# Sum of squares in the recurrent branch's output norm: fp32r products on split squares in place of plain fp32 products

## The chip, the cores and the metric

One core of a Trainium2 chip runs the whole program. The metric is the device time of one execution in microseconds; the median over the runs is given. The engines are TensorE (PE in the profile, its weight loads PEld), VectorE (DVE), ScalarE (ACT), GpSimd (POOL) and SyncE (SP), which only issues DMAs here. They run side by side and wait for each other by semaphores; within one engine, instructions run in the order in which they are written.

## The reference, cut to what matters

The model is a decoder trunk of width 1024 over 1024 positions. Layer 0 mixes with two head groups side by side: windowed attention (A) and gated linear attention (B, the recurrent branch, 4 heads of width 128). The change touches the norm on B's output:

```python
def rms_norm(x, g):
    xf = x.astype(jnp.float32)
    y = xf * lax.rsqrt(jnp.mean(xf * xf, axis=-1, keepdims=True) + EPS)
    return (y * g.astype(jnp.float32)).astype(x.dtype)
...
    ob = gla(split_heads(qb, N_HEADS_B), split_heads(kb, N_HEADS_B),
             split_heads(vb, N_HEADS_B), split_heads(log_a, N_HEADS_B))
    ob = rms_norm(ob, g_out_b) * jax.nn.silu(split_heads(rb, N_HEADS_B).astype(jnp.float32))
```

The mean runs over the 128 channels of one head. This happens once per execution, for 4 heads.

## The kernel before, in words

All activations lie transposed: 128 channels on the partitions, 1024 positions along the row. The large projections split both operands into a high fp32r part and a low rest, and make each product of 512 columns out of three fp32r products (high by high, low by high, high by low; `cross` for whole tiles, `half_tile` for half tiles). ScalarE or GpSimd makes the high part, VectorE or GpSimd the low one. Weights come by DMA into `w_raw` and GpSimd splits them, one tile of 128x1024 after the other: L594 writes `w_hi`, L597 writes `w_lo`. There are two slots for split tiles, so the split of tile n+2 starts when TensorE has ended its products with tile n.

Branch B works on two heads at a time (`bp` 0, then 1; `h` 0 and 1 within it). For each pair TensorE projects k, q, v (twice) and r (twice), and in between makes the gates, the running sums of the decay ("cum"), transposes of the decayed keys ("kd") and of v ("vt"), states ("kv"), scores ("att"), outputs ("o") and the sums of squares ("ss"). The list `B_SEQ` fixes that order and gives each result one of four PSUM slots of two banks; `slot_free` makes TensorE wait until VectorE has taken what lay in the slot before. So `b_project("r", 1, 1)`, which uses slot 3, waits until `take_gate(1, 0)` has taken the result of `b_project("r", 1, 0)` from slot 3.

The norm runs so: VectorE copies the output out of PSUM (`take_bo`, L1560), ScalarE squares it (`b_square`, L2186) into `b_v` (h = 0) or `b_att` (h = 1), TensorE multiplies a 128x128 matrix of ones with the squares (`out_squares`, L946), which leaves each position's sum on all partitions; VectorE scales it (`out_var`, L1565), ScalarE takes the logarithm and the exponential for a first guess of the root (`b_guess`, `b_root`), and VectorE refines it in steps (`out_step`: L1573, L1577, L1579), then applies gain and gate (L1582, L1586).

For pair 0, TensorE's order around it is: `chunk_out(0)`, `b_project("v", 1, 0)`, `gate(1)`, `out_squares(0, 0)`, `out_squares(0, 1)`, `b_project("v", 1, 1)`, `cumulate(1)`, `b_project("r", 1, 0)`, `kd_transposes(1)` (L886), `bv_transposes` twice (L893), `b_project("r", 1, 1)`. `kd_transposes(1)` waits for `b_kd` (L1510), which VectorE makes in `decays(1)` after `log_sigmoid(1)`, `out_var`, `log_decay(1)`, six steps of `out_step` and `take_bv(1, 1)`:

```python
                dve.wait_ge(B.e, 6 * bp + 3)
                dve.tensor_tensor(b_kd[:], b_k[bp][:], b_e[:], ALU.mult).then_inc(B.dec, 1)

                dve.wait_ge(B.dec, 6 * bp + 2)
                dve.tensor_tensor(chunks(b_e[:]), chunks(b_cum[:]), at(b_cum[:], CH // 2 - 1), ALU.subtract).then_inc(B.dec, 1)
                take_gate(bp, 0)
```

For pair 1, branch A's first head pair is woven in: its projections are 50 "pieces" (0 to 15 make v, 16 and 17 transpose it, 18 to 25 make the first half of k, "K0", 26 to 33 the first half of q, "Q0", 34 to 41 and 42 to 49 the second halves "K1" and "Q1"). A piece of a projection is three products of 512 columns (L1028, L1029, L1030). Before, the squares of pair 1 stand between pieces 33 and 34, and `scores(0)`, the first attention scores, between pieces 41 and 42; `scores(0)` waits until `out_var(1, 1)` has emptied the slot. VectorE's order there is `take_bo(1, 0)`, `take_bo(1, 1)`, `take_part(0, Q0)` (rotates Q0 and splits it, L1650 to L1665; it waits for piece 33), `out_var(1, 0)`, `out_var(1, 1)`, then the first step on K1.

Of the kernel before, what the change touches and what calls it, by code (L numbers as in the profile page):

```python
# [22 lines left out]
F32 = mybir.dt.float32  # L23
F32R = mybir.dt.float32r
# [69 lines left out]
def build(nc, xT, pos, consts, logmul, gains, wgu, bgu, wgl, w_in, w_out, w_u, w_v, w_outc, wsT, bsp,  # L94
          w_up, w_dn, conv, outT):
    with ExitStack() as ctx:
        arena = -(-nc.sbuf_base // 64) * 64

        def sb(name, kb, shape, dt=F32):
            return nc.alloc_sbuf_tensor_at(name, shape, dt, offset=arena + int(kb * 1024))  # L100

        def sem(name):
            return ctx.enter_context(nc.semaphore(name))
# [10 lines left out]
        acc = sb("acc", 180, [P, S])  # L114
        cst = sb("cst", 200, [P, C_N])
        gain = sb("gain", 202.25, [P, G_N])
        ones = sb("ones", 202.5, [P, P])
        cw = sb("cw", 203, [P, 2, 2 * FT, 4])
        tiny = sb("tiny", 204.5, [P, 64])
        carry = sb("carry", 204.75, [P, 4])  # L120
# [43 lines left out]
        b_st = sb("b_st", 144, [P, NCH, P])  # L164
        b_att = sb("b_att", 172, [P, S])
        b_v = sb("b_v", 180, [P, S])
        wgu_sb = sb("wgu_sb", 205, [P, 256])
        wgl_raw = sb("wgl_raw", 188, [P, KT, 16])
        wgl_both = sb("wgl_both", 206, [P, KT, 48], F32R)
# [60 lines left out]


        s_wgl = sem("w_gl_split")
        s_eps = sem("eps_written")

        class Bsem:
            def __init__(self):
                self.ready = sem("b_result_ready")
                self.free = sem("b_result_taken")
                self.silu = sem("b_silu")
                self.gl = sem("b_gl_projected")  # L240
                self.glt = sem("b_gl_taken")
                self.min = sem("b_min")
                self.e = sem("b_exp_ln")
                self.la = sem("b_log_decay")
                self.dec = sem("b_decay_steps")
                self.state = sem("b_state")
                self.zero = sem("b_scores_zeroed")
                self.osq = [sem("b_out0_squared"), sem("b_out1_squared")]
                self.oe = [sem("b_out0_ln_exp"), sem("b_out1_ln_exp")]
                self.o = [sem("b_out0_steps"), sem("b_out1_steps")]  # L250
        B = Bsem()
# [204 lines left out]
        def _(sp):  # L456
# [11 lines left out]
            sp.dma_start(cw[:], conv).then_inc(s_tab, 16)  # L468
            sp.dma_start(pos_i[:], pos.partition_broadcast(P)).then_inc(s_tab, 16)
            sp.dma_start(lmul[:], logmul).then_inc(s_tab, 16)  # L470
            sp.wait_ge(s_setup, 2)
            sp.dma_start(wgu_sb[0:16, :], wgu).then_inc(s_tab, 16)
            sp.dma_start(wgu_sb[32:48, :], wgu).then_inc(s_tab, 16)
            sp.dma_start(wgu_sb[48:49, :], bgu).then_inc(s_tab, 16)
# [238 lines left out]
        def b_out(kind, bp, a=0):  # L713
            slot = B_SEQ[b_index(kind, bp, a)][3]
            return ps[:, 2 * slot:2 * slot + 2, :].rearrange("p b n -> p (b n)")
# [95 lines left out]
        def _(pe):  # L811
# [128 lines left out]

            def out_squares(bp, h):
                slot_free("ss", bp, h)
                pe.wait_ge(B.osq[h], bp + 1)
                t = b_v if h == 0 else b_att
                for c in range(2):
                    ins = pe.matmul(b_out("ss", bp, h)[:, c * HALF:(c + 1) * HALF], ones[:], t[:, c * HALF:(c + 1) * HALF],  # L946
                                    start=True, stop=True)
                ins.then_inc(B.ready, 1)


# [197 lines left out]
            for j in range(16, 26):  # L1148
                piece(0, j)
            chunk_out(1)  # L1150
            for j in range(26, 34):
                piece(0, j)
            out_squares(1, 0)
            out_squares(1, 1)
            for j in range(34, 42):
                piece(0, j)
            pe.wait_ge(*b_taken(len(B_SEQ) - 1))
            scores(0)
# [234 lines left out]
        def _(dve):  # L1393
# [30 lines left out]
                                         act_hi[:, k, :].bitcast(F32), ALU.mult, ALU.subtract).then_inc(norm.lo.sem, 1)  # L1424

            dve.memset(ones[:], 1.0).then_inc(s_setup, 1)
            dve.memset(tiny[:, 61:62], EPS).then_inc(s_eps, 1)
            dve.memset(wgu_sb[0:32, :], 0.0).then_inc(s_setup, 1)
            dve.memset(glT[32:64, :], 1.0).then_inc(s_rope_v, 1)
            for k in range(KT):  # L1430
# [30 lines left out]
            def reduce_angles():  # L1461
                for part in PI_PARTS:
                    step(dve.scalar_tensor_tensor(r_a[:], r_n[:], -part, r_a[:], ALU.mult, ALU.add))
                step(dve.tensor_scalar(r_a[:], r_a[:], 3.1415925, -3.1415925, ALU.min, ALU.max))
# [23 lines left out]
            def take_bv(bp, h):  # L1488
                if bp:
                    dve.wait_ge(*b_count("vt", bp - 1, 1))  # L1490
                dve.tensor_tensor(b_vt[:, h, :], ready("v", bp, h), rstd[:], ALU.mult).then_inc(B.free, 1)
# [67 lines left out]
            def take_bo(bp, h):  # L1559
                dve.tensor_copy((b_k if h == 0 else b_q)[bp][:], ready("o", bp, h)).then_inc(B.free, 1)  # L1560

            def out_var(bp, h):

                v = out_variance(h)
                dve.tensor_scalar(v, ready("ss", bp, h), 1.0 / P, EPS, ALU.mult, ALU.add).then_inc(B.free, 1)  # L1565

            def out_step(bp, h, step):

                v, y, o = out_variance(h), out_guess(bp, h), (b_k if h == 0 else b_q)[bp]
                c0 = 5 * bp  # L1570
                if step == 0:
                    dve.wait_ge(B.oe[h], 2 * bp + 2)
                    dve.scalar_tensor_tensor(v, v, -0.5, y, ALU.mult, ALU.mult).then_inc(B.o[h], 1)  # L1573
                    return
                dve.wait_ge(B.o[h], c0 + step)
                if step == 1:
                    dve.tensor_tensor(v, v, y, ALU.mult).then_inc(B.o[h], 1)  # L1577
                elif step == 2:
                    dve.scalar_tensor_tensor(y, v, 1.5, y, ALU.add, ALU.mult).then_inc(B.o[h], 1)  # L1579
                elif step == 3:  # L1580
                    dve.wait_ge(B.osq[h], bp + 1)
                    dve.scalar_tensor_tensor(o[:], o[:], gain[:, G_OUT:G_OUT + 1], y, ALU.mult, ALU.mult).then_inc(B.o[h], 1)  # L1582
                else:
                    dve.wait_ge(B.silu, 2 * bp + h + 1)
                    r = oT[:, 4 + 2 * bp + h, :]
                    dve.tensor_tensor(r, o[:], r, ALU.mult).then_inc(B.o[h], 1)  # L1586
# [19 lines left out]
            take_bo(0, 0)  # L1606
            take_bo(0, 1)
            reduce_angles()
            take_bv(1, 0)
            log_sigmoid(1)  # L1610
            out_var(0, 0)
# [111 lines left out]
            take_bo(1, 0)  # L1723
            take_bo(1, 1)
            take_part(0, Q0)
            out_var(1, 0)
            out_var(1, 1)
            take_part(0, K1, (0,))
# [407 lines left out]
        def _(act):  # L2136
# [46 lines left out]

            def b_square(bp, h):
                act.wait_ge(*b_taken(b_index("o", bp, h)))
                act.activation((b_v if h == 0 else b_att)[:], (b_k if h == 0 else b_q)[bp][:], ACT.Square  # L2186
                               ).then_inc(B.osq[h], 1)

            def b_guess(bp, h):
                act.wait_ge(*b_taken(b_index("ss", bp, h)))  # L2190
# [155 lines left out]
            def ffn(F, layer, norm, nxt, last):  # L2346
# [107 lines left out]
                silu(FT - 1)  # L2454
                for t in range(4, STEPS):
                    if last and t == ITEM_AT[0] - 3:
                        act.wait_ge(s_eps, 1)
                        act.activation(tiny[:, 62:63], tiny[:, 61:62], ACT.Abs_reciprocal_sqrt).then_inc(s_preload, 1)
                    d_high(t)
                    if t in ITEM_AT:  # L2460
                        i = ITEM_AT.index(t)
                        if last:
                            act.wait_ge(*past(F.dsum, len(SUMS)))
                            act.wait_ge(*past(F.xadd, tile_done(0, HALF_TILES[0][i])))
                            half_square(f1, 0, i)
                        else:
                            item(0, i)
# [134 lines left out]
```

## Time and profile before

| | before |
|---|---|
| median of 3 runs | 2119.1 us (2119.04 to 2119.45) |
| the profiled execution | 2119.03 us; its span, first to last instruction, 2117.2 us |
| mean granted TensorE clock | 0.997 |
| TensorE busy | 2091.2 us, 99% of the span |
| VectorE busy | 1467.6 us, 69% |
| ScalarE busy | 881.0 us, 42% |
| GpSimd busy | 885.6 us, 42% |

The busy time of an engine is the sum of its instructions' durations with overlaps counted once. The profiled execution is one run of its own; it lies 0.07 us under the median, so sums made on its trace can be set against the median as they stand. The squares of pair 0 stand near 140 us of the span and those of pair 1 near 219 us.

### The profile page before, as it was taken

How to read it: one execution, taken by the hardware profiler on the slowest of the kernel's cores; microseconds unless marked ns; L12 is line 12 of the kernel's file. 1: busy time of each engine (PE TensorE's matmuls, PEld its weight loads, DVE VectorE, ACT ScalarE, POOL GpSimd, SP SyncE). 2: the span in 40 equal slices, each digit the busy share in tenths (PEclk: the TensorE clock that was granted, in tenths of full speed). 3: DMA queues.
4: the chain of work that ended last, by engine and by line, in shares of the span. 5: the costliest groups of instructions: out<-in, count | busy, mean ns of one | idle time of the engine just before them, and what ended most of it. 6: DMA issues, size and time to landing. Idle time of an engine off the chain costs nothing.

```text
span 2117.2 us, 26181 instructions
## 1 busy us (share of the span) xinstructions
PE 2091.2 (99%) x10190; PEld 1709.3 (81%) x10190; DVE 1467.6 (69%) x1631; ACT 881.0 (42%) x1154; POOL 885.6 (42%) x459
## 2 busy tenths in 40 slices
PE   8999999999999999999999999999999999999997
PEld 6888777778888888888888888888888888888886
DVE  7669855554986677667899604437966676686988
ACT  4231344453554444444435431215544444444444
POOL 4333221223488767770001333434877768730000
PEclk9999999999999999999999999999999999999999
DMA  4101000021422222117984111213222222239872
GB/s 170 41 30 41 30 23 19 21 80 61 146 93 80 90 90 80 70 70 251 389 300 163 60 41 41 60 40 119 81 89 90 90 72 78 90 124 384 306 279 80
DMA packets 95100, 236.10 MB, mean 112 GB/s; under 512 B 10081, under 2 KB 12418, under 8 KB 94978
## 3 DMA queue, kind: packets, MB, share of 16 engines
q1 hardware_dynamic: 93106, 229.70, 30.5%
q10 hardware_dynamic: 1872, 4.74, 0.6%
q8 instruction: 81, 1.33, 0.3%
q14 instruction: 41, 0.34, 0.0%
HBM read 198.75 MB, written 35.65 MB: 111 GB/s over the span
## 4 chain that ended last, share of the span: by engine, by line
PE 90%; DVE 6%; issue 2%; ACT 2%; DMA 0%; POOL 0%; SPq 0%; DVEq 0%; ACTq 0%; POOLq 0%
PE ps L1228 12%; PE ps L1229 12%; PE ps L1230 12%; PE ps L1262 7%; PE ps L1264 7%; PE ps L1265 7%; PE ps L818 5%; PE ps L821 5%; PE ps L824 5%; PE ps L1028 2%; PE ps L1030 2%; PE ps L1029 2%; PE ps L1133 2%; PE ps L1098 1%; PE ps L1333 1%
## 5 line engine op out<-in xcount | busy, mean ns | idle before, releaser
L594 POOL TENSOR_TENSOR w_hi<-w_raw,ones 128x1024 fp32r<-128x1024 f32 x56 | 115.6, 2065 | 746.4 <-PE ps L824 232.1
L1228 PE MATMUL ps<-t_hi,w_hi 128*128 128x512 f32 x672 | 264.1, 393 | 1.6 <-ACT snap L2365 1.3
L1229 PE MATMUL ps<-t_lo,w_hi 128*128 128x512 f32 x672 | 262.0, 390 | 0.0
L1230 PE MATMUL ps<-t_hi,w_lo 128*128 128x512 f32 x672 | 261.6, 389 | 0.0
L1262 PE MATMUL ps<-d_hi 128*128 128x512 f32 (+1 forms) x640 | 244.6, 382 | 0.7 <-DVE d_lo L1941 0.7
L1264 PE MATMUL ps<-d_lo,d_hi 128*128 128x512 f32 (+1 forms) x640 | 243.9, 381 | 0.0
L1265 PE MATMUL ps<-d_hi,d_lo 128*128 128x512 f32 (+1 forms) x640 | 243.9, 381 | 0.0
L645 POOL TENSOR_TENSOR w_lo<-w_sum,w_hi 128x1024 fp32r<-128x1024 f32 x84 | 232.3, 2776 | 25.2 <-ACT w_hi L2368 25.2
L645 POOL TENSOR_TENSOR w_lo<-w_raw,w_hi 128x1024 fp32r<-128x1024 f32 x84 | 157.5, 1875 | 172.1 <-ACT w_hi L2368 158.3
L1228 PE MATMUL ps<-act_hi,w_hi 128*128 128x512 f32 x504 | 196.2, 389 | 0.0
L1229 PE MATMUL ps<-act_lo,w_hi 128*128 128x512 f32 x504 | 196.1, 389 | 0.0
L1230 PE MATMUL ps<-act_hi,w_lo 128*128 128x512 f32 x504 | 196.1, 389 | 0.0
L818 PE MATMUL ps<-act_hi,w_hi 128*128 128x512 f32 x592 | 185.0, 394 | 1.2 <-DVE b_st L1541 0.6
L821 PE MATMUL ps<-act_lo,w_hi 128*128 128x512 f32 x592 | 182.4, 389 | 0.0
L824 PE MATMUL ps<-act_hi,w_lo 128*128 128x512 f32 x592 | 182.4, 389 | 0.0
L1228 PEld LDWEIGHTS ps<-t_hi,w_hi 128*128 128x128 f32 x672 | 126.1, 188 | 36.0 <-ACT snap L2365 10.0
L2368 ACT ACTIVATE w_hi<-w_sum 128x1024 fp32r<-128x1024 f32 x84 | 89.2, 1061 | 151.5 <-PE ps L1230 112.3
L597 POOL TENSOR_TENSOR w_lo<-w_raw,w_hi 128x1024 fp32r<-128x1024 f32 x56 | 149.3, 2665 | 4.4
L2352 ACT ACTIVATE ps<-fz,cw 128x1024 f32<-128x1024 f32 x88 | 105.5, 1201 | 106.0 <-DVE fz L1906 99.8
L1230 PEld LDWEIGHTS ps<-t_hi,w_lo 128*128 128x128 f32 x672 | 126.2, 188 | 26.7
L1229 PEld LDWEIGHTS ps<-t_lo,w_hi 128*128 128x128 f32 x672 | 126.2, 188 | 25.6
L1898 DVE TENSOR_TENSOR fz<-ps,snap 128x512 f32<-128x512 f32 x40 | 27.6, 691 | 169.5 <-PE ps L1230 169.5
(307 smaller groups left out, 4503.7 us busy)
## 6 DMA issues: line engine op xcount, KB each, us to landing
w_raw<-w_up SPq DMA_DIRECT2D x44, 1024.0 KB, 5.0
d_ring<-w_dn SPq DMA_DIRECT2D x146, 256.0 KB, 7.9
d_ring<-g_kept SPq DMA_DIRECT2D x124, 256.0 KB, 9.6
g_kept<-gst SPq DMA_DIRECT2D x44, 512.0 KB, 2.6
w_raw<-w_in SPq DMA_DIRECT2D x24, 512.0 KB, 3.5
chain_a<-g_kept SPq DMA_DIRECT2D x44, 256.0 KB, 8.7
x_kept<-x SPq DMA_DIRECT2D x16, 512.0 KB, 8.3
x<-x_kept SPq DMA_DIRECT2D x16, 512.0 KB, 10.5
```

The lines of the kernel that those rows point to most:

```text
L594: pool.tensor_tensor(w_hi[:, slot, :], w_raw[:, parity, :], ones[:, 0:1].to_broadcast([P, 1024]), ALU.mult).then_inc(s_whi, 1)
L597: pool.tensor_tensor(w_lo[:, slot, :], w_raw[:, parity, :], w_hi[:, slot, :].bitcast(F32), ALU.subtract).then_inc(s_wsplit, 1)
L645: pool.tensor_tensor(w_lo[:, slot, cols].rearrange("p (a j c) -> p a j c", j=4, c=P), src, w_hi[:, slot, cols].bitcast(F32).rearrange("p ( ...
L818: pe.matmul(out[:, cols], wh, act_hi_k[:, cols], start=first, stop=False)
L821: pe.matmul(out[:, cols], wh, act_lo_k[:, cols], start=False, stop=False)
L824: ins = pe.matmul(out[:, cols], wl, act_hi_k[:, cols], start=False, stop=last)
L1228: pe.matmul(out, wh, bh, start=(fresh and j == 0), stop=False, skip_group_check=True)
L1229: pe.matmul(out, wh, bl, start=False, stop=False, skip_group_check=True)
L1230: ins = pe.matmul(out, wl, bh, start=False, stop=(j == 3), skip_group_check=True)
L1262: pe.matmul(out, w[:, 0, wcols], w[:, 1, cols], start=(s == 0 and i not in (D6, D7)), stop=False, skip_group_check=True)
L1264: pe.matmul(out, w[:, 0, wcols], g[:, 1, cols], start=False, stop=False, skip_group_check=True)
L1265: return pe.matmul(out, g[:, 0, wcols], w[:, 1, cols], start=False, stop=(s == NBLK - 1), skip_group_check=True)
```

## The change

The squares are written in two parts, as the projections' operands are: ScalarE makes `b_sq_hi`, the squares rounded to fp32r, with one more Copy for each head; VectorE makes `b_sq_lo`, the squares less the high part, in place over the squares (`square_low`, new). TensorE multiplies ones in fp32r with the high part and then with the low part into the same PSUM bank: 4 fp32r products for each head instead of 2 plain fp32 ones. `square_low` for pair 0 stands in VectorE's order after `reduce_angles()`, for pair 1 after `take_part(0, Q0)`; TensorE's `out_squares` for pair 1 moves three pieces later, behind piece 36. The matrix of ones becomes an fp32r tile, which all other users read as plain fp32. One semaphore (`s_eps`) is merged into `s_setup`.

```diff
-        ones = sb("ones", 202.5, [P, P])
+        ones_r = sb("ones_r", 202.5, [P, P], F32R)
+        ones = ones_r[:].bitcast(F32)
...
+        b_sq_hi = [sb(f"b_sq_hi{h}", scr[6 + h], [P, S], F32R) for h in range(2)]
+        b_sq_lo = [sb("b_sq_lo0", 180, [P, S], F32R), sb("b_sq_lo1", 172, [P, S], F32R)]
...
-            sp.wait_ge(s_setup, 2)
+            sp.wait_ge(s_setup, 3)
...
             def out_squares(bp, h):
                 slot_free("ss", bp, h)
-                pe.wait_ge(B.osq[h], bp + 1)
-                t = b_v if h == 0 else b_att
-                for c in range(2):
-                    ins = pe.matmul(b_out("ss", bp, h)[:, c * HALF:(c + 1) * HALF], ones[:], t[:, c * HALF:(c + 1) * HALF],
-                                    start=True, stop=True)
+                pe.wait_ge(B.osq[h], 2 * bp + 2)
+                for part in (b_sq_hi[h], b_sq_lo[h]):
+                    if part is b_sq_lo[h]:
+                        pe.wait_ge(B.sqlo, 2 * bp + h + 1)
+                    for c in range(2):
+                        cols = slice(c * HALF, (c + 1) * HALF)
+                        ins = pe.matmul(b_out("ss", bp, h)[:, cols], ones_r[:], part[:, cols], start=part is b_sq_hi[h],
+                                        stop=part is b_sq_lo[h])
                 ins.then_inc(B.ready, 1)
...
-            for j in range(26, 34):
+            for j in range(26, 37):
                 piece(0, j)
             out_squares(1, 0)
             out_squares(1, 1)
-            for j in range(34, 42):
+            for j in range(37, 42):
                 piece(0, j)
...
-            dve.memset(tiny[:, 61:62], EPS).then_inc(s_eps, 1)
+            dve.memset(tiny[:, 61:62], EPS).then_inc(s_setup, 1)
...
+            def square_low(bp, h):
+
+                t = b_v if h == 0 else b_att
+                dve.wait_ge(B.osq[h], 2 * bp + 2)
+                dve.tensor_tensor(b_sq_lo[h][:], t[:], b_sq_hi[h][:].bitcast(F32), ALU.subtract).then_inc(B.sqlo, 1)
...
             reduce_angles()
+            square_low(0, 0)
+            square_low(0, 1)
             take_bv(1, 0)
...
             take_part(0, Q0)
+            square_low(1, 0)
+            square_low(1, 1)
             out_var(1, 0)
             out_var(1, 1)
...
             def b_square(bp, h):
                 act.wait_ge(*b_taken(b_index("o", bp, h)))
-                act.activation((b_v if h == 0 else b_att)[:], (b_k if h == 0 else b_q)[bp][:], ACT.Square
-                               ).then_inc(B.osq[h], 1)
+                t = b_v if h == 0 else b_att
+                act.activation(t[:], (b_k if h == 0 else b_q)[bp][:], ACT.Square).then_inc(B.osq[h], 1)
+                act.wait_ge(B.osq[h], 2 * bp + 1)
+                act.activation(b_sq_hi[h][:], t[:], ACT.Copy).then_inc(B.osq[h], 1)
```

## Rows read from the trace of the kernel before

**Rows 1.** The page: busy time of each engine, and the chain that ended last.

```profile
...
PE 2091.2 (99%) x10190; PEld 1709.3 (81%) x10190; DVE 1467.6 (69%) x1631; ACT 881.0 (42%) x1154; POOL 885.6 (42%) x459
...
PE 90%; DVE 6%; issue 2%; ACT 2%; DMA 0%; POOL 0%; SPq 0%; DVEq 0%; ACTq 0%; POOLq 0%
...
```

**Rows 2.** TensorE's waits over the span: waiting line, releaser, total, times, longest.

```profile
...
PE ps L1113 <- DVE tiny L1677: 1.0, 1, 1.0
...
```

**Rows 3.** TensorE from 6 us, in order of time: start, duration, line, operation.

```profile
...
6.20 1.06 PE L959 MATMUL ps<-act_hi,wgl_both 128*48 128x512 f32 x2 [6.20 <-ACT act_hi L2145]
...
15.10 0.62 PE L959 MATMUL ps<-act_hi,wgl_both 128*48 128x512 f32 x2
...
```

**Rows 4.** The line of the sums of squares: durations, least, median, most.

```profile
...
L946 PE MATMUL ps<-b_v,ones x8: 591/592/697, 140.6 to 220.1; 128*128 128x512 f32 x8
...
```

**Rows 5.** VectorE in order of time from 127 to 184 us.

```profile
...
138.87 1.22 DVE L1491 TENSOR_TENSOR b_vt<-ps,rstd 128x1024 f32<-128x1024 f32 x1 [3.21 <-PE ps L824]
...
154.66 1.22 DVE L1573 SCALAR_TENSOR_TENSOR b_v<-b_v,glT 128x1024 f32<-128x1024 f32 x1
155.91 2.80 DVE L1577 TENSOR_TENSOR b_v<-b_v,glT 128x1024 f32<-128x1024 f32 x1
158.74 3.31 DVE L1579 SCALAR_TENSOR_TENSOR glT<-b_v,glT 128x1024 f32<-128x1024 f32 x1
...
166.70 1.23 DVE L1510 TENSOR_TENSOR b_kd<-b_k,b_e 128x1024 f32<-128x1024 f32 x1 [1.13 <-ACT b_e L2172]
167.96 1.23 DVE L1513 TENSOR_TENSOR b_e<-b_cum 128x1024 f32<-128x1024 f32 x1
169.10 1.22 DVE L1523 TENSOR_TENSOR oT<-ps,rstd 128x1024 f32<-128x1024 f32 x1
...
```

**Rows 6.** ScalarE in order of time from 127 to 184 us.

```profile
...
135.69 1.06 ACT L2207 ACTIVATE ropeS<-r_a 128x1024 f32<-128x1024 f32 x1 [4.58 <-DVE r_a L1464]
...
```

**Rows 7.** GpSimd in order of time from 120 to 232 us.

```profile
...
138.82 1.89 POOL L594 TENSOR_TENSOR w_hi<-w_raw,ones 128x1024 fp32r<-128x1024 f32 x1 [14.08 <-PE ps L824]
...
155.33 2.29 POOL L594 TENSOR_TENSOR w_hi<-w_raw,ones 128x1024 fp32r<-128x1024 f32 x1 [12.18 <-PE ps L824]
157.70 3.26 POOL L597 TENSOR_TENSOR w_lo<-w_raw,w_hi 128x1024 fp32r<-128x1024 f32 x1
168.01 2.92 POOL L594 TENSOR_TENSOR w_hi<-w_raw,ones 128x1024 fp32r<-128x1024 f32 x1 [7.05 <-PE ps L824]
...
```

**Rows 8.** TensorE in order of time from 166 to 175 us.

```profile
...
167.31 0.61 PE L824 MATMUL ps<-act_hi,w_lo 128*128 128x512 f32 x2
168.07 1.06 PE L886 MATMUL ps<-cst,b_kd 128*128 128x128 f32 x8
...
170.63 0.70 PE L818 MATMUL ps<-act_hi,w_hi 128*128 128x512 f32 x2
...
```

**Rows 9.** TensorE in order of time from 213 to 223 us.

```profile
...
213.57 0.40 PE L1029 MATMUL ps<-act_lo,w_hi 128*128 128x512 f32 x1
...
218.35 0.39 PE L1029 MATMUL ps<-act_lo,w_hi 128*128 128x512 f32 x1
...
218.80 1.88 PE L946 MATMUL ps<-b_v,ones 128*128 128x512 f32 x4
...
222.47 0.40 PE L1029 MATMUL ps<-act_lo,w_hi 128*128 128x512 f32 x1
...
```

**Rows 10.** VectorE in order of time from 200 to 237 us.

```profile
...
219.01 0.73 DVE L1650 STREAM_SHUFFLE a_sh<-ps 128x512 f32<-128x512 f32 x1
...
222.29 0.69 DVE L1665 TENSOR_TENSOR a_ql<-a_sh,a_qh 128x512 fp32r<-128x512 f32 x1
222.90 1.22 DVE L1565 TENSOR_SCALAR b_st<-ps 128x1024 f32<-128x1024 f32 x1
...
```

**Rows 11.** Two lines with fp32r output: durations, least, median, most.

```profile
...
L1708 DVE TENSOR_TENSOR act_lo<-oT,act_hi x8: 1202/1224/2059, 432.0 to 470.8; 128x1024 fp32r<-128x1024 f32 x8
...
L2368 ACT ACTIVATE w_hi<-w_sum x84: 1042/1062/1066, 569.1 to 1870.0; 128x1024 fp32r<-128x1024 f32 x84
...
```

More of the change, by code:

```diff
@@ L232, in build @@
         s_wgl = sem("w_gl_split")
-        s_eps = sem("eps_written")
         class Bsem:
@@ L248, in __init__ @@
                 self.osq = [sem("b_out0_squared"), sem("b_out1_squared")]
+                self.sqlo = sem("b_out_squares_low")
                 self.oe = [sem("b_out0_ln_exp"), sem("b_out1_ln_exp")]
@@ L1580, in out_step @@
                 elif step == 3:
-                    dve.wait_ge(B.osq[h], bp + 1)
+                    dve.wait_ge(B.osq[h], 2 * bp + 2)
                     dve.scalar_tensor_tensor(o[:], o[:], gain[:, G_OUT:G_OUT + 1], y, ALU.mult, ALU.mult).then_inc(B.o[h], 1)
@@ L2456, in ffn @@
                     if last and t == ITEM_AT[0] - 3:
-                        act.wait_ge(s_eps, 1)
+                        act.wait_ge(s_setup, 2)
                         act.activation(tiny[:, 62:63], tiny[:, 61:62], ACT.Abs_reciprocal_sqrt).then_inc(s_preload, 1)
```

## The prediction

> **What bounds the kernel now.** I read the page first: TensorE is busy 99% of the span and makes up 90% of the chain that ended last [rows 1]. After the start it almost never waits: its longest later wait is 1.0 us [rows 2]. So what counts is time added to or taken from TensorE's own row of work, and every other engine counts only where TensorE would stand and wait for it. Next I read the two places of the squares in order of time, engine by engine [rows 5 to 10]. The reader is to see two things there. Near 168 us TensorE and VectorE arrive almost together: `kd_transposes(1)` starts at 168.07, and `b_kd`, for which it waits, ended at 166.70 + 1.23 = 167.93 [rows 5, 8]. TensorE's last product before it started near 167.31 + 0.23, so it could have gone on at about 167.77; it was already waiting 0.3 us. And near 219 us VectorE has just begun four microseconds of rotation [rows 10] when TensorE reaches the squares at 218.80 [rows 9].
>
> **The products.** A fp32r product of 512 columns takes one start interval: seven pieces of three products from 213.57 to 218.35 give 4.78 / 21 = 0.228 us [rows 9]. A plain fp32 product appears as two rows (4 for a head's two products); from 218.80 to 222.47 lie eight of them and one fp32r product, so each is (3.67 - 0.23) / 8 = 0.43 us [rows 9]; its shown duration of 592 ns overlaps the next one's [rows 4]. One pair of heads costs 8 x 0.43 = 3.44 us before and 8 x 0.228 = 1.82 us after. TensorE's work falls by 1.62 us for each pair, 3.24 us in all. If nothing waited, the time would be 2119.1 - 3.2 = 2115.9 us, or 0.15% less, which is under what a measurement of this kernel can tell from no change; I take 0.2% (4.24 us) as that bound.
>
> **ScalarE's and VectorE's added work.** Four Copies to fp32r cost 1.06 us each, four subtractions 1.22 us each, by the same forms on other lines [rows 11]. For pair 0 both are covered: ScalarE is idle 4.58 us before its 135.69 [rows 6], for 2.1 us of Copies; VectorE is idle 3.21 us before 138.87 [rows 5], for about 2.4 us of `square_low`. Without that cover `take_bv(1, 0)`, and all that VectorE does behind it, would slip by those 2.4 us. TensorE comes to the squares at 140.6 [rows 4], after both. For pair 1 ScalarE's Copies end before 219 us, so they too cost nothing there; VectorE's do not (below). The merged semaphore makes SyncE wait for the same memset as before; zero.
>
> **Pair 0: the saved time is lost at `kd_transposes(1)`.** From `gate(1)` on, VectorE's chain to `b_kd` does not run through the squares' end: VectorE takes the gates, then has its own queue of log, variance and `out_step`. So `b_kd` does not come earlier, while TensorE comes 1.62 us earlier, at about 166.15. At best it waits until 168.07 as before, and the gain of pair 0 is zero.
>
> It gets worse through GpSimd. Its split of the next weights starts when TensorE ends `b_project("r", 1, 0)`: at 168.01 now, at 166.39 after. Look at what happens when GpSimd's split and a VectorE instruction with two SBUF inputs meet. L594 issued at 155.33 while L1573 ran until 155.88; it ended at 157.62, 1.74 us after that. L1577 issued at 155.91 and ended 1.09 us after L594. L597 issued at 157.70 and ended at 160.96, 2.25 us after L1577; L1579 issued at 158.74 and ended 1.09 us after L597 [rows 5, 7]. Alone L594 takes 1.89 us, and beside a VectorE instruction that reads PSUM neither is slowed (the instructions at 138.82 and 138.87) [rows 5, 7]. They take turns, each whole. The Trainium skill says so too (SBUF — State Buffer, section "SBUF: two separate sides"): the port pair shared by VectorE and GpSimd is an exclusive lock held for the whole instruction, and the loser blocks. By that rule the trace agrees; a shared bandwidth would instead let both run slowly, and the loss below would come out nearer 1.2 us than 3.4 us.
>
> Now the new order. L594 issues at 166.39, 0.31 us before `b_kd` at 166.70, and holds until 166.39 + 1.89 = 168.28. `b_kd` ends at 168.28 + 1.09 = 169.37; `kd_transposes(1)` starts 0.14 us later, at 169.51. L597 has been queued since 168.36. VectorE's next, L1513, waits for `b_kd` and issues 0.03 us after it, as L1577 and L1579 did after theirs, and both lost that race; so L597 runs to 169.37 + 2.25 = 171.62, and L1513 ends at 172.71. Behind L1513 stands `take_gate(1, 0)` (L1523; it began 0.09 us before L1513's end), ending at 172.62 + 1.22 = 173.84. `b_project("r", 1, 1)` needs that slot: it starts at 173.98 instead of 170.63. TensorE's two transposes between take 170.63 - 168.07 = 2.56 us, so it is ready at 172.07 and waits. **Loss at pair 0: 3.35 us.** ScalarE's exponentials and VectorE's copies also stand behind L1513, but `b_project("r", 1, 1)` covers them: it is long, and they meet no further split. From there all that follows is triggered by TensorE, so it shifts as a whole.
>
> **Pair 1: the low part comes late.** Three pieces more put the squares at 218.80 + 9 x 0.228 = 220.85 (in times of before, shift aside). The high products of h = 0 end at 221.3. But `square_low(1, 0)` stands behind `take_part(0, Q0)`, which starts at 219.01, when Q0 is done, and gives the engine free at 222.90, where L1565 now starts [rows 10]. So it runs 222.90 to 224.12 and the second to about 225.26. TensorE waits from 221.3 to 224.26, then pays about 0.2 us for a weight load not overlapped (my estimate: a load and product after a wait start 0.14 us after the releaser, and L818 after the transposes took 0.70 us against 0.61 to 0.62 us [rows 8]). The low pair of h = 0 and the high pair of h = 1 end at 225.37; the low pair of h = 1 is ready by 225.40 and ends at 225.86. Five pieces (3.42 us) end at 229.28. Before, eight pieces followed from 222.24 and ended at 227.71. **Loss at pair 1: 1.6 us**, that is 3.2 us of waiting less 1.62 us saved. Behind it, `out_var(1, 1)` ends near 227.6, before `scores(0)` at 229.3.
>
> **Sum.** 3.35 + 1.6 = 4.95 us. The profiled execution took 2119.03 us, so 2124.0; against the median 2119.1 that is **2124.1 us, 0.23% slower**. Bounds: pair 0 from 0 (no collision) over 1.45 (`b_kd` held, L1513 not) to 3.6; pair 1 from 1.3 to 1.9. I take the upper case for pair 0 because both times that GpSimd was queued before a dependent VectorE instruction, GpSimd went first.
>
> **The rivals.**
> - *L1513 wins its race*: pair 0 loses 169.51 + 2.56 - 170.63 = 1.44 us; sum 3.0, 2122.1 us. For it: 0.03 us is all that decides.
> - *No collision (not slower by the bound)*: `b_kd` issues before L594. It decides at one point, whether TensorE's end of `b_project("r", 1, 0)` plus 0.2 us comes before 166.70. It needs a shift of TensorE under 1.3 us or a VectorE chain 0.3 us earlier. Then pair 0 gives 0 and the sum is 1.6: 2120.7 us. Against it: both ends of that 0.31 us hang on work that the change does not touch, apart from the 1.62 us worked out above.
> - *The saving shows, or part of it*: the chain to `b_kd` is early enough, and the low squares come in time. The rows at 166.70 and 222.90 speak against both; one of them alone gives 2117 to 2119 us, both 2115.9.
> - *The clock falls during a wait.* TensorE would stand 3.3, 1.9 and 3.0 us, longer than anywhere after its start [rows 2]. At the start pairs of products took 1.06 us against 0.62 us later [rows 3], start intervals nearly doubled; the page of the profile shows no fall afterwards. If some 3 to 7 us of products ran at half rate once more, 1.5 to 3.5 us come on top: about 2126.5 us. The Trainium skill (TensorE: Matmul & The Clock Gate, section "What's actually happening") says that an idle array goes back to 1.2 GHz; no row here shows it for waits of this length.
>
> **How the numbers follow.** Chances: my forecast 0.54, L1513 first 0.11, no collision 0.13, saving in whole or part 0.12, clock 0.10. The likeliest case alone spans 2123.4 to 2124.9. The range 2120.4 to 2126.6 takes in the forecast, the first two rivals and most of the clock case; below lie the saving's cases. Slower by over 0.2% means over 2123.3: most of the forecast case (0.47, since half a microsecond may be given back downstream) and the clock, 0.56. Faster by over 0.2% needs under 2114.9, which no sum here reaches: 0.02. Within: 0.42.
>
> **What would show it.** In the profile after: L946 as 8 rows per pair 0.228 us apart; L594 before `b_kd` near 166.4 and L1510 at some 2.7 us instead of 1.23; L1513 at over 3 us; `b_project("r", 1, 1)` starting near 174; TensorE's waits naming L1510 and L1523. At pair 1 a wait of 3 us for VectorE inside L946's group, near 224.6 with the shift on top. I am wrong if L1510 keeps 1.23 us, or if TensorE's waits by the squares are short, or if more collisions of GpSimd and VectorE change downstream than I assume, which is none.

## The result, and the profile after

| | before | changed |
|---|---|---|
| median, 9 runs each | 2119.04 us | 2123.87 us |
| range | 2117.97 to 2122.59 us | 2123.56 to 2128.31 us |
| the profiled execution | 2119.03 us | 2123.66 us |
| ratio, 95% interval | | 1.0028 (1.002 to 1.0037) |

The forecast was 2124.1 us. The page of the changed kernel shows little: TensorE's busy time fell by 1.8 us (2091.2 in [rows 1]) while the time rose, and VectorE's part of the chain went from 6% to 7%.

```profile
PE 2089.4 (98%) x10190; PEld 1711.6 (81%) x10190; DVE 1468.3 (69%) x1635; ACT 884.9 (42%) x1158; POOL 884.3 (42%) x459
...
PE 89%; DVE 7%; issue 2%; ACT 2%; DMA 0%; POOL 0%; SPq 0%; DVEq 0%; ACTq 0%; POOLq 0%
```

TensorE's waits show it at once. The longest after the start was 1.0 us before [rows 2]; now two of 3.2 and 2.7 us stand ahead of it (waiting line, releaser, total, times, longest):

```profile
PE ps L889 <- DVE b_kd L1516: 3.2, 1, 3.2
PE ps L952 <- DVE b_sq_lo L1572: 2.7, 1, 2.7
...
PE ps L1119 <- DVE tiny L1691: 1.0, 1, 1.0
```

**Pair 0.** VectorE in order of time (compare [rows 5]):

```profile
139.02 1.22 DVE L1497 TENSOR_TENSOR b_vt<-ps,rstd 128x1024 f32<-128x1024 f32 x1 [0.79 <-PE ps L827]
...
154.84 2.92 DVE L1585 SCALAR_TENSOR_TENSOR b_v<-b_v,glT 128x1024 f32<-128x1024 f32 x1
157.79 3.31 DVE L1589 TENSOR_TENSOR b_v<-b_v,glT 128x1024 f32<-128x1024 f32 x1
...
167.00 2.55 DVE L1516 TENSOR_TENSOR b_kd<-b_k,b_e 128x1024 f32<-128x1024 f32 x1 [1.12 <-ACT b_e L2188]
169.58 3.26 DVE L1519 TENSOR_TENSOR b_e<-b_cum 128x1024 f32<-128x1024 f32 x1
172.77 1.21 DVE L1529 TENSOR_TENSOR oT<-ps,rstd 128x1024 f32<-128x1024 f32 x1
```

GpSimd in order of time ([rows 7]):

```profile
153.89 2.78 POOL L597 TENSOR_TENSOR w_hi<-w_raw,ones_r 128x1024 fp32r<-128x1024 f32 x1 [10.52 <-PE ps L827]
...
166.57 1.89 POOL L597 TENSOR_TENSOR w_hi<-w_raw,ones_r 128x1024 fp32r<-128x1024 f32 x1 [6.56 <-PE ps L827]
168.54 3.21 POOL L600 TENSOR_TENSOR w_lo<-w_raw,w_hi 128x1024 fp32r<-128x1024 f32 x1
```

TensorE ([rows 8]):

```profile
165.88 0.61 PE L827 MATMUL ps<-act_hi,w_lo 128*128 128x512 f32 x2
169.69 1.70 PE L889 MATMUL ps<-cst,b_kd 128*128 128x128 f32 x8 [3.20 <-DVE b_kd L1516]
171.18 2.99 PE L896 MATMUL ps<-cst,b_vt 128*128 128x128 f32 x16
174.03 0.73 PE L821 MATMUL ps<-act_hi,w_hi 128*128 128x512 f32 x2
```

Twice a GpSimd instruction of the split goes ahead of a VectorE instruction that TensorE's next step hangs on; these are the two races that the forecast took as lost. First, the high half of the split (L597) issues at 166.57, 0.43 us before `b_kd` (L1516) at 167.00, and ends at 168.46; `b_kd` ends 1.09 us later, at 169.55. Second, the low half (L600), queued at 168.54, goes ahead of L1519, issued at 169.58, and ends at 171.75. L1519 ends 1.09 us later, `take_gate(1, 0)` (L1529) ends at 173.98, and `b_project("r", 1, 1)` starts at 174.03. TensorE could have begun the transposes at about 166.35. New against the forecast: the 24 transposes took 4.34 us instead of 2.56 [rows 8].

**Pair 1.** VectorE ([rows 10]), then TensorE ([rows 9]):

```profile
216.71 1.22 DVE L1566 COPY b_k<-ps 128x1024 f32<-128x1024 f32 x1 [0.74 <-PE ps L939]
...
225.67 0.69 DVE L1679 TENSOR_TENSOR a_ql<-a_sh,a_qh 128x512 fp32r<-128x512 f32 x1
226.28 1.22 DVE L1572 TENSOR_TENSOR b_sq_lo<-b_v,b_sq_hi 128x1024 fp32r<-128x1024 f32 x1
...
234.28 0.74 DVE L1664 STREAM_SHUFFLE a_sh<-ps 128x512 f32<-128x512 f32 x1
```

```profile
224.22 0.61 PE L952 MATMUL ps<-b_sq_hi,ones_r 128*128 128x512 f32 x2
227.56 0.88 PE L952 MATMUL ps<-b_sq_lo,ones_r 128*128 128x512 f32 x2 [2.73 <-DVE b_sq_lo L1572]
228.23 1.05 PE L952 MATMUL ps<-b_sq_hi,ones_r 128*128 128x512 f32 x2
229.09 1.05 PE L952 MATMUL ps<-b_sq_lo,ones_r 128*128 128x512 f32 x2
```

`square_low` (L1572) begins at 226.28, when the rotation's last instruction ends; TensorE did the high products at 224.22 and stood until 227.56. Then its products start 0.43 us apart (the next instruction after the last pair began at 229.94, so 4 products took 1.71 us from 228.23 on), nearly twice the 0.228 us of [rows 9]. The reason is in the granted clock, the last but two of the columns here (stretch, length, busy time and count of TensorE, its weight loads, VectorE, ScalarE, GpSimd, then the clock as a share of full speed, DMA share, GB/s), changed kernel:

```profile
170.00:173.40 3.40, 3.40 (x18) 3.40 (x17) 3.40 (x2) 0.52 (x1) 1.76 (x1) 0.50 0.22 40
228.00:231.40 3.40, 3.40 (x10) 2.59 (x9) 2.99 (x3) 1.06 (x1) 0.00 (x0) 0.50 0.00 0
1214.40:1217.80 3.40, 3.40 (x17) 2.58 (x16) 0.73 (x1) 0.00 (x0) 0.00 (x0) 1.00 0.00 0
```

Behind each of the two waits TensorE ran at 1.2 instead of 2.4 GHz for some 3.4 us. The kernel before had one such stretch itself, with TensorE 100% busy, and 16 products of one column each ended 1.3 us ahead of it. The changed kernel's profile has no fall there.

```profile
1214.40:1217.80 3.40, 3.40 (x10) 2.62 (x9) 0.10 (x1) 3.34 (x9) 0.00 (x0) 0.51 0.00 0
```

```profile
1211.22 1.94 PE L1354 MATMUL ps<-ones,rstd 1*128 1x1 f32 x16
```

So the stages have to be compared one by one. VectorE's starts mark them: `take_bv(1, 0)` (138.87 in [rows 5]), `take_bo(1, 0)`, and the first step on K1. The latter two, before:

```profile
213.33 1.22 DVE L1560 COPY b_k<-ps 128x1024 f32<-128x1024 f32 x1 [0.74 <-PE ps L936]
...
227.90 0.74 DVE L1650 STREAM_SHUFFLE a_sh<-ps 128x512 f32<-128x512 f32 x1
```

Before, pair 0's stage takes 213.33 - 138.87 = 74.46 us and pair 1's 227.90 - 213.33 = 14.57 us. Changed: 216.71 - 139.02 = 77.69 and 234.28 - 216.71 = 17.57 us. Losses: 3.2 us and 3.0 us. TensorE's products, matched one by one between the two profiles, lie 0.15 us later at the start of pair 0's stage, 6.38 us later behind pair 1 and 6.27 us later just ahead of 1214 us. Behind that stretch they lie 4.66 us later, since the missing fall gives 1.6 us back: 0.15 + 3.2 + 3.0 - 0.1 - 1.6 = 4.65 us, against 2123.66 - 2119.03 = 4.63 us measured.

### The profile page after: what moved, and what is told of

It is laid out like the page before. It is cut to its first block, busy times and chain, and to the rows that moved or that the text cites. A ratio compares the mean times of both kernels' runs of the same rounds, so it can differ in the third digit from the quotient of the medians.

```text
span 2121.9 us, 26190 instructions
## 1 busy us (share of the span) xinstructions
PE 2089.4 (98%) x10190; PEld 1711.6 (81%) x10190; DVE 1468.3 (69%) x1635; ACT 884.9 (42%) x1158; POOL 884.3 (42%) x459
## 4 chain that ended last, share of the span: by engine, by line
PE 89%; DVE 7%; issue 2%; ACT 2%; DMA 0%; POOL 0%; SPq 0%; DVEq 0%; ACTq 0%; POOLq 0%
PE ps L1234 12%; PE ps L1235 12%; PE ps L1236 12%; PE ps L1268 7%; PE ps L1270 7%; PE ps L1271 7%; PE ps L821 5%; PE ps L827 5%; PE ps L824 5%; PE ps L1034 2%; PE ps L1036 2%; PE ps L1035 2%; PE ps L1139 2%; PE ps L1104 1%; PE ps L1119 1%
## 5 line engine op out<-in xcount | busy, mean ns | idle before, releaser
L597 POOL TENSOR_TENSOR w_hi<-w_raw,ones_r 128x1024 fp32r<-128x1024 f32 x56 | 113.2, 2022 | 753.6 <-PE ps L827 235.8
L600 POOL TENSOR_TENSOR w_lo<-w_raw,w_hi 128x1024 fp32r<-128x1024 f32 x56 | 149.2, 2664 | 4.4
```

What stands on the lines that cost most here:

```text
L597: pool.tensor_tensor(w_hi[:, slot, :], w_raw[:, parity, :], ones[:, 0:1].to_broadcast([P, 1024]), ALU.mult).then_inc(s_whi, 1)
L600: pool.tensor_tensor(w_lo[:, slot, :], w_raw[:, parity, :], w_hi[:, slot, :].bitcast(F32), ALU.subtract).then_inc(s_wsplit, 1)
```

## The experiments

For each profiled execution the two stages were measured in the same way, as differences from the kernel before. The last column tells where a stretch at half clock begins; the one that every profile has in its last 8 to 11 us is left out, and so is the start, where the kernel before has its products nearly twice as far apart up to 12.9 us. Half clock means 1.2 GHz. The kernel before, run beside the experiments, had medians of 2118.87 (e1 to e4), 2118.83 (e5 to e8) and 2119.01 us (e9 to e11); beside e12 it ran once, in 2117.54 us.

| kernel | median us (runs) | pair 0 | pair 1 | half clock near |
|---|---|---|---|---|
| before | 2119.04 (9) | 0 | 0 | 1214 |
| changed | 2123.87 (9) | +3.2 | +3.0 | 170, 228 |
| e1, pair 0 alone | 2121.54 (11) | +3.4 | 0.0 | 171 |
| e2, split held | 2122.07 (11) | +0.1 | +1.6 | 1217 |
| e3, wait filled | 2123.67 (11) | +3.2 | +1.6 | 1220 |
| e4, low part first | 2121.25 (11) | +3.4 | -1.6 | 173, 1217 |
| e5, low split held | 2124.84 (7) | +3.2 | +3.2 | 171, 229 |
| e6, pair 1 alone | 2120.99 (10) | 0.0 | +3.0 | 224 |
| e7, both mended | 2114.45 (11) | -2.0 | -1.6 | none |
| e8, changed again | 2124.41 (7) | +3.3 | +1.6 | 1220 |
| e9, before, keys early | 2119.58 (11) | -0.4 | 0.0 | none |
| e10, as e5 | 2127.71 (1) | +3.2 | +3.2 | 173, 231 |
| e11, before again | 2119.26 (1) | 0.0 | 0.0 | none |
| e12, as e5 | 2126.41 (1) | +3.1 | +3.0 | 171, 229, 1222 |

The medians scatter more than the stages. A half-clock stretch comes or goes, and `take_bv(1, 0)` starts anywhere from 138.87 to 141.19 us. Behind the two stages the distance to the kernel before drifts too: in e8 it shrinks by 0.9 us between 1225 and 1600 us, in e10 it grows by 1.2 us between 1225 us and the end; why is not known. Where the two disagree by a microsecond, the stages of a profile are the firmer reading.

### e1: pair 0 alone

```diff
-            square_low(1, 0)
-            square_low(1, 1)
...
-            for j in range(26, 37):
+            for j in range(26, 34):
                 piece(0, j)
```

with plain fp32 products on `b_v` and `b_att` for `bp == 1` and no second Copy there.

> Pair 0 as in the changed kernel, pair 1 as before (plain fp32 squares, old place, no low part). Theory (collision at pair 0, late low part at pair 1, each its own loss): b_kd waits for GpSimd's split, b_project r(1,1) starts about 3.2 us later than before, nothing else differs near 219 us; median 2119.0 + 3.2 = 2122.2 us. Rival (one common cost, such as VectorE's and ScalarE's added instructions or fp32r squares as such): half of the 4.8 us, 2121.4 us, with b_kd at its 1.23 us. Rival (all the loss at pair 1): 2117.4 to 2119 us.

2121.54 us, ratio 1.0012 (1.0003 to 1.0021). Pair 0 loses 3.4 us, pair 1 nothing, `b_kd` takes 2.56 us. The losses are separate; the rival of a common cost falls, and so does that of all at pair 1. By the median alone the common cost (2121.4 us) would have fitted better than the theory (2122.2 us).

### e6: pair 1 alone

The same split the other way: plain products for `bp == 0`, and no `square_low(0, h)`.

> Pair 1 as in the changed kernel, pair 0 as before. Theory: pair 0 costs nothing, b_kd at 1.23 us; at pair 1 TensorE waits 2.7 us for the low part, which costs 1.6 us when the granted clock stays high and 3.0 us when it falls behind the wait: 2120.6 or 2122.0 us. Rival (pair 1's loss needs pair 0's delay): 2119 us or less.

2120.99 us, ratio 1.0013 (1.0004 to 1.0022), between the two expected. Pair 0 stands at 0.0, `b_kd` at 1.23 us, pair 1 at +3.0 us with a half-clock stretch.

### e2: GpSimd's split waits for the keys

```diff
-            with pool.Fori(0, N_A // 2 + 1) as i:
-                for t in range(2):
-                    looped(2 + t, i, 2, t, (s_proj, i * 2 + (t + 1)))
+            for n in range(2, N_A + 4):
+                plain(n, n % 2, (s_proj, n - 1), *(((B.dec, 8),) if n == N_A else ()))
```

> The changed kernel with one more wait on GpSimd: the split of weight tile 12 starts only when b_kd is done (GpSimd's loop written out, same instructions). Theory (GpSimd's split, released early, holds b_kd and then L1519): b_kd takes 1.23 us again, the transposes of the keys start near 168.2 instead of 169.7 and r(1,1) near 170.8 instead of 174.0, so 3.2 us less than the changed kernel: 2120.6 us. Rival (b_kd is late for some other reason, the chain before it): no change, 2123.8 us. Rival (only b_kd's own delay counts): 1.5 us less, 2122.3 us.

VectorE and then GpSimd of this kernel:

```profile
167.85 1.23 DVE L1515 TENSOR_TENSOR b_kd<-b_k,b_e 128x1024 f32<-128x1024 f32 x1 [1.12 <-ACT b_e L2187]
169.11 1.23 DVE L1518 TENSOR_TENSOR b_e<-b_cum 128x1024 f32<-128x1024 f32 x1
```

```profile
169.25 2.84 POOL L597 TENSOR_TENSOR w_hi<-w_raw,ones_r 128x1024 fp32r<-128x1024 f32 x1 [8.39 <-DVE b_kd L1515]
```

`b_kd` is back at 1.23 us, its successor too, and pair 0's loss went from 3.2 to 0.1 us. The only other edit is GpSimd's loop written out; e5 has it too and keeps the loss, so the early split is the cause of the loss of 3.2 us at pair 0. The gain of 1.62 us does not appear even so: TensorE waits 1.9 us for `b_kd`, where it had waited 0.3 us. The median, 2122.07 us (ratio 1.0015, 1.0006 to 1.0024), is 1.5 us above the expected 2120.6 and nearer the rival of one race; the stage decides here.

### e5, e10, e12: only the low half of the split waits

```diff
                 pool.wait_ge(s_whi, done)
+                if isinstance(done, int) and done == N_A + 2:
+                    pool.wait_ge(B.dec, 9)
```

on GpSimd, in `split`, the loop written out as in e2. `B.dec` reaches 9 when L1519 of the changed kernel (L1520 here) is done.

> The changed kernel with GpSimd's loop written out, where only the second half of the split of tile 12 (L600, the low part) waits until VectorE's L1519 is done. This takes the second lost race away and leaves the first. Theory (two races, each taken whole): b_kd still takes 2.5 us, L1519 takes 1.2 instead of 3.3 us, take_gate(1, 0) ends near 172.0 instead of 174.0. If the granted clock stays high behind the wait of 3.2 us, r(1,1) starts 1.5 us after its place before (1.8 us less than the changed kernel, 2122.1 us); if it falls to half as in the changed kernel's profile, the 24 transposes take 4.3 us instead of 2.6 and r(1,1) starts where it did in the changed kernel, and the time stays at 2123.8 us. Rival (only one cause, the collision with b_kd, matters and the clock nothing): 2122.1 us with transposes of 2.6 us in either case.

> The kernel of e5 for another profile. Theory: if no stretch at half clock follows the wait for b_kd in this execution, the 24 transposes take 2.6 us and r(1,1) starts 1.5 us after its place before; if one does, they take over 4 us and it starts 3.2 us after. Rival: r(1,1) starts in the same place in both cases.

> The kernel of e5 and e10 for a third profile, since both earlier ones had a stretch at half clock behind the wait for b_kd. Theory: without such a stretch the 24 transposes take 2.6 us and r(1,1) starts 1.5 us after its place before; with one, 3.2 us after. Rival: the same place in both cases.

VectorE and TensorE of e5:

```profile
166.89 2.62 DVE L1517 TENSOR_TENSOR b_kd<-b_k,b_e 128x1024 f32<-128x1024 f32 x1 [1.12 <-ACT b_e L2189]
169.55 1.23 DVE L1520 TENSOR_TENSOR b_e<-b_cum 128x1024 f32<-128x1024 f32 x1
170.69 1.22 DVE L1530 TENSOR_TENSOR oT<-ps,rstd 128x1024 f32<-128x1024 f32 x1
```

```profile
169.66 1.06 PE L890 MATMUL ps<-cst,b_kd 128*128 128x128 f32 x8 [3.27 <-DVE b_kd L1517]
170.56 3.36 PE L897 MATMUL ps<-cst,b_vt 128*128 128x128 f32 x16
173.57 1.01 PE L822 MATMUL ps<-act_hi,w_hi 128*128 128x512 f32 x2
```

The second race is gone (1.23 us at 169.55, where the changed kernel has 3.26), `take_gate(1, 0)` ends at 171.91, and yet `b_project("r", 1, 1)` gains nothing: the transposes ran at half clock, 3.9 us for the 24. All three profiles had that stretch, so the case without it was not seen, and these runs alone do not tell the race's own price. e8 does. The times are no help: e5's median of 2124.84 us is above the 2122.1 and the 2123.8 us expected. The single runs of e10 and e12, 2127.71 and 2126.41 us, begin the stages 2.3 and 1.0 us later than the kernel before; e12 has a stretch near 1222 us besides, and e10 the drift named above.

### e8: the changed kernel again

> The changed kernel once more, unaltered, for a second profile. Theory (which stretches at half clock appear depends on where the execution stands when TensorE has waited, and so differs from one execution to the next): the waits of 3.2 us and 2.7 us and b_kd's 2.55 us return unchanged, the stretches at half clock need not be the same ones, and the loss at pair 1 is 1.6 us without one and 3.0 us with one. Rival (the clock follows the program alone): the same two stretches of 3.4 us behind the two waits, none near 1217 us.

TensorE near 170 us, and two stretches with their clock:

```profile
169.94 1.06 PE L889 MATMUL ps<-cst,b_kd 128*128 128x128 f32 x8 [3.20 <-DVE b_kd L1516]
170.84 1.91 PE L896 MATMUL ps<-cst,b_vt 128*128 128x128 f32 x16
174.29 0.73 PE L821 MATMUL ps<-act_hi,w_hi 128*128 128x512 f32 x2 [1.54 <-DVE oT L1529]
```

```profile
228.00:231.40 3.40, 3.40 (x15) 2.52 (x16) 3.18 (x3) 1.24 (x2) 0.00 (x0) 1.00 0.00 0
1219.60:1223.00 3.40, 3.40 (x10) 2.63 (x9) 0.04 (x1) 3.34 (x9) 0.00 (x0) 0.50 0.00 0
```

Same kernel, same waits (3.2 and 2.7 us), no half-clock stretch behind either. The transposes take 1.06 and 1.91 us, as before, and TensorE then waits 1.54 us for `take_gate(1, 0)` (L1529): that is the second race's price at full clock. Pair 0 loses 3.3 us all the same. Pair 1 loses 1.6 us. The half-clock stretch lies near 1220 us instead, and the time is 2123.73 us, 0.07 us from the first profile's. So the rival that the clock follows the program alone falls.

### e11: the kernel before again

> The kernel before, unaltered, for another profile. Theory (the stretch at half clock near 1214 us hangs on the execution's phase and not on the program): it may be there or not; where it is missing the time from 1210 to 1225 us shrinks by 1.7 us. Rival (it belongs to the program): it is there at the same place.

```profile
1216.60:1220.00 3.40, 3.40 (x17) 2.82 (x16) 0.00 (x0) 3.33 (x9) 0.44 (x1) 1.00 0.02 5
```

The same place in the program as 1214.4 to 1217.8 in the first profile, here at full clock (with `take_bv(1, 0)` 2.2 us later). That stretch belongs to an execution and needs no wait. The same 16 products of one column, 1.9 us in which TensorE counts as busy, stand ahead of it here too, at 1213.17 us, and nothing follows; so what decides is not shown.

### e3: the wait filled with products

```diff
                 pe.wait_ge(B.osq[h], 2 * bp + 2)
+                for n in range(12 if bp == 1 and h == 0 else 0):
+                    cols = slice((n % 2) * HALF, (n % 2 + 1) * HALF)
+                    pe.matmul(b_out("ss", bp, h)[:, cols], ones_r[:], b_sq_hi[h][:, cols], start=True, stop=True)
```

> The changed kernel with 12 more fp32r products of ones with the high squares ahead of the pair 1 squares of head 0 (2.7 us of work whose result is overwritten by the same value), so that TensorE works through the time in which it would wait for the low part. Theory (the wait made the granted clock fall to 1.2 GHz for 3.4 us behind it, which cost 1.7 us at pair 1): no stretch at half clock near 228 us, products 0.228 us apart there, scores(0) 1.7 us earlier, 2122.1 us although TensorE does more. Rival (the clock's fall there comes from something else, or costs nothing): time unchanged or up to 0.3 us longer, 2123.8 to 2124.1 us.

```profile
224.78 2.88 PE L949 MATMUL ps<-b_sq_hi,ones_r 128*128 128x512 f32 x12
227.50 0.61 PE L955 MATMUL ps<-b_sq_hi,ones_r 128*128 128x512 f32 x2
228.12 0.73 PE L955 MATMUL ps<-b_sq_lo,ones_r 128*128 128x512 f32 x2
```

Full clock behind it, pair 1 at +1.6 us. The theory's 2122.1 us did not come. But e2 and e8 waited 2.7 us without filling and had no half-clock stretch either, so this does not show that the filling kept the clock up. The median (2123.67 us, ratio 1.002, 1.0011 to 1.0029) is that of the changed kernel. Inconclusive on the clock; it shows only that 2.7 us of extra products there cost nothing.

### e4: the low part ahead of the rotation

```diff
+            square_low(1, 0)
+            square_low(1, 1)
             take_part(0, Q0)
-            square_low(1, 0)
-            square_low(1, 1)
```

> The changed kernel with VectorE's two square_low of pair 1 ahead of take_part(0, Q0), where VectorE stood idle 3.3 us. Theory (TensorE waits at pair 1 only because the low part is queued behind the rotation of Q0): no wait at the squares, no half clock near 228 us; the rotation of Q0 ends 1.1 us later, which makes scores(0) wait for out_var by up to 0.5 us; scores(0) some 4.1 us earlier than in the changed kernel, 2119.7 us. Rival (the later rotation costs as much, since the first scores and the exponentials stand behind it): 2 us gained at most, 2121.8 us or more.

VectorE and TensorE:

```profile
222.40 1.23 DVE L1572 TENSOR_TENSOR b_sq_lo<-b_v,b_sq_hi 128x1024 fp32r<-128x1024 f32 x1 [1.09 <-ACT b_sq_hi L2205]
224.44 1.22 DVE L1572 TENSOR_TENSOR b_sq_lo<-b_att,b_sq_hi 128x1024 fp32r<-128x1024 f32 x1 [0.81 <-ACT b_sq_hi L2205]
```

```profile
226.46 0.62 PE L952 MATMUL ps<-b_sq_hi,ones_r 128*128 128x512 f32 x2
...
227.82 0.62 PE L952 MATMUL ps<-b_sq_lo,ones_r 128*128 128x512 f32 x2
```

Both low parts are there by 225.66, TensorE arrives at 226.46 and passes without a wait. Pair 1 turns from +1.6 or +3.0 into -1.6 us: the whole saving of the products. 2121.25 us, ratio 1.0012 (1.0003 to 1.0021), is 1.5 us above the expected 2119.7 and 0.6 us under the rival's 2121.8. Here too the stage decides; the two stages give 3.4 - 1.6 = 1.8 us over the kernel before, the median 2.4.

### e7: both places mended by order

```diff
-            for step_n in range(3):
-                out_step(0, 1, step_n)
+            out_step(0, 1, 0)
             take_bv(1, 1)
             decays(1)
...
+                if bp:
+                    out_step(0, 1, 1)
                 dve.wait_ge(B.e, 6 * bp + 3)
                 dve.tensor_tensor(b_kd[:], b_k[bp][:], b_e[:], ALU.mult).then_inc(B.dec, 1)
+                if bp:
+                    out_step(0, 1, 2)
```

and the edit of e4.

> The changed kernel with both places mended by order alone: square_low of pair 1 ahead of take_part(0, Q0), and on VectorE, for pair 0's norm of head 1, step 0 ahead of take_bv(1, 1), step 1 between the subtraction and the wait for ScalarE's exponential, step 2 behind b_kd, so that b_kd ends about 163.8 instead of 169.6. Same instructions as the changed kernel on every engine. Theory (TensorE's saving is real and was only lost in waits): the transposes of the keys start near 166.3 without a wait, r(1,1) 1.9 us earlier than before; pair 1 gives 1.6 us; 2119.0 - 3.5 = 2115.5 us, faster than both kernels. Rival (the saving is not to be had, since the next wait, for take_gate(1, 0) or for the exponentials behind it, takes its place): 2117.4 us or more.

```profile
162.44 1.23 DVE L1518 TENSOR_TENSOR b_kd<-b_k,b_e 128x1024 f32<-128x1024 f32 x1
```

```profile
166.38 1.03 PE L889 MATMUL ps<-cst,b_kd 128*128 128x128 f32 x8
...
168.91 0.71 PE L821 MATMUL ps<-act_hi,w_hi 128*128 128x512 f32 x2
```

`b_kd` is made at 162.44, the transposes start at 166.38 with no wait, `b_project("r", 1, 1)` at 168.91. Pair 0 -2.0, pair 1 -1.6 us. 2114.45 us, ratio 0.9979 (0.997 to 0.9988): faster than both kernels, with every instruction of the changed one, and 1.1 us under the expected 2115.5. The profile's 2113.94 us is lower than the stages give, since no half-clock stretch fell near 1214 us.

### e9: the kernel before with the keys early

The edit of e7 in `decays` and in VectorE's order of pair 0, on the kernel before.

> The kernel before (plain fp32 squares, its own places) with VectorE's order of pair 0 changed as in e7: b_kd early. It tells how much of e7's gain is the order alone. Theory (TensorE waited 0.3 us for b_kd before, so the order alone gives that much and the rest of e7 is the squares' saving): 2118.8 - 0.3 = 2118.5 us, transposes of the keys at 167.8 without a wait. Rival (the new order is worth several us by itself): 2116 us or less.

2119.58 us, ratio 1.0 (0.9991 to 1.0009); pair 0 -0.4 us by the stages, and no gain by the median (expected 2118.5 us). In the profile the transposes start at 167.92 with no wait, so by the stages the order alone is worth what TensorE had waited for `b_kd`. Of e7's 2.0 us at pair 0 the other 1.6 us are the change itself, once nothing waits.

## Why the prediction was right, point by point

- **Products.** Forecast 0.228 us for a fp32r product in place of each 0.43 us row of a plain one (two rows for a product), 1.62 us for a pair of heads. e4 and e7 show the 1.6 us at pair 1; e7 shows 2.0 us at pair 0, which is 1.62 and the 0.3 us of the old wait. Right.
- **Covered work.** `square_low` of pair 0 ran at 135.87 to 138.23 in VectorE's idle time, and `take_bv(1, 0)` kept its place behind TensorE. Right.
- **Pair 0.** Forecast 3.35 us, measured 3.1 to 3.4 in the eight profiles with it. The two lost races came as drawn: with the 0.15 us taken off by which this execution starts later, `b_kd` ended 0.03 us from the drawn time and `take_gate` 0.01 us. e2 took the cause away and the loss with it. The sum had no half-clock stretch on the transposes; where one came, it hid in the wait for `take_gate`.
- **Pair 1.** Forecast 1.6 us, measured 1.6 us in e2, e3 and e8, but 3.0 to 3.2 us where the clock fell (changed kernel, e5, e6, e10, e12). The mechanism was right; the term left out the clock. The forecast also has the rotation already begun when TensorE reaches the squares, while its own rows put the one at 219.01 and the other at 218.80; nothing in the sum hangs on it.
- **The clock** had been a rival with a chance of 0.10. It took part in the first profile and still the sum came out, since the kernel before had one of its own that was missing here: 1.4 us more at pair 1 against 1.6 us less near 1214 us. That is luck: nothing in the forecast ties the two together. So 2124.1 against 2123.87 us is closer than the working deserves. The forecast read from the page that the clock does not fall after the start. The page gives it in 40 slices of 53 us, in which 3.4 us do not show; its own trace had the stretch at 1214 us. Both kernels have such stretches in some executions, and each stretch found near 1214 us moved the time by 1.6 us.
- **Downstream.** In the changed kernel's first profile the shift of 6.38 us behind pair 1 was still 6.27 us near 1200 us. "Shifts as a whole" held there; over the rest of the program other profiles drifted by up to 1.2 us (above), which the forecast did not have.
- **Left open.** How often the clock falls behind a wait of 3 us was not counted; six of eight profiles with the wait at pair 0 had it, and five of the seven in which TensorE stood 2.7 us at pair 1, too few to tell what decides. The second race without a half-clock stretch was seen only through the waits of 1.5 us in e8 and e3, not by removing it.

## What to carry to other kernels

When an engine that bounds a kernel is made faster, ask first what its end releases: here the saving of 1.6 us at pair 0 went into a longer wait for the keys (e2), and GpSimd's split, released 1.6 us earlier and so 0.4 us ahead of the one VectorE instruction that mattered, added a loss of 3.2 us. The place of a helper instruction in its engine's queue is worth as much as its length: with `square_low` behind the rotation pair 1 lost 1.6 us or more, and with it ahead of the rotation pair 1 kept its whole saving of 1.6 us. And compare kernels stage by stage when a difference is a few microseconds out of 2119, because a stretch at half clock can hide one or be taken for one.

## What the runs showed of the hardware

- GpSimd's split, once queued, went ahead even of a VectorE instruction with SBUF inputs that issued back to back. In the changed kernel L597 was queued from 153.89; VectorE's L1585 issued at 154.84, before its predecessor had ended, and took 2.92 us instead of the 1.22 us of before [rows 5].
- A stretch of some 3.4 us at 1.2 GHz followed waits of 2.7 and 3.2 us in some executions and not in others of the same kernel, and in six of the 14 profiles one came near 1214 to 1222 us. The Trainium skill (TensorE: Matmul & The Clock Gate, section "What's actually happening") speaks of idle time as what brings the half rate. Here the same wait of 2.7 us brought it in the changed kernel's first profile and not in e8, and near 1214 us, with TensorE busy throughout, it came in the first profile of the kernel before and not in e11.
